# Two transformer stacks on one core: norms worked out by token tile behind the last pieces of the stage before, the token scale moved to the feed-forward's output, and new step orders

## The chip, the cores and the metric

The kernel runs on one core of a Trainium2 chip. A core has TensorE (PE, matrix products into eight PSUM banks), VectorE (DVE), ScalarE (ACT), GpSimd (POOL) and SyncE (SP, which issues transfers here); each follows its own list of instructions and they wait for each other by semaphores. The metric is the device time of one execution in microseconds, the median of the runs.

## The reference, cut to what matters

```python
def rms_norm(x, g):                      # x: 256 tokens x 1024, fp32
    return x * rsqrt(mean(x * x) + EPS) * g

for l in range(2):                       # first block
    x = x + 0.5 * swiglu(rms_norm(x, ffn1_norm[l]), w1, w3, w2)   # (silu(h@w1) * (h@w3)) @ w2, 2816 wide
    h = rms_norm(x, mix_norm[l]); z = h @ w_in[l]                 # 6752 columns
    ...                                  # neighbourhood attention, gated linear attention, latent attention
    x = x + mixed @ w_out[l]
    x = x + 0.5 * swiglu(rms_norm(x, ffn2_norm[l]), ...)
for l in range(2):                       # second block
    z = rms_norm(x, norm_g[l]) @ w_in_2[l]
    ...                                  # forgetting attention, convolution, compressed and sparse attention
    x = x + mixed @ w_out_2[l]
return rms_norm(x, final_g)
```

All of it is fp32. There are nine norms: three in each first layer, one in each second layer, one at the end.

## The kernel before, in words

All tokens stay in `x`, as two tiles of 128 tokens (t = 0, 1). A product in fp32 precision is made of three passes with operands split in a high and a low part (`passes`). Weights come in units of 1 MB through a ring of three slots (`Ring`): SP loads a unit into `raw` once the low part of the unit three before is made, ScalarE makes the high part (`hi`, line 391) once TensorE has used that slot, VectorE the low part (`lo`, line 402).

A norm (`Norm`) goes: ScalarE squares a tile and sums it; GpSimd makes 1/sqrt in two steps; VectorE scales the tile into `X`; TensorE transposes 8 pieces of each tile into four banks (`pe_transposes`); ScalarE writes the high part of each of the 8 blocks of 256 tokens, times the gain (`act_high`), and VectorE the low part (`dve_low`). The next stage waits for these block by block.

A feed-forward (`FFN`) goes over 11 pairs of units: w1 and w3 (`up_unit`, 48 matmuls of 256 columns each), then the w2 unit of the pair before (`down_unit`, 24 matmuls of 512). ScalarE makes Silu from PSUM, VectorE the product, both the high and low part of the hidden. The sums of x += 0.5 * result are four adds of 128x512 (`dve_add`).

The mixers run by orders written out by hand, one list for each engine (`PE1`, `ACT1`, `DVE1` for the first block's, `PE2`, `ACT2`, `DVE2` for the second's). A step is named with its number; a step that waits holds up all steps behind it in its list. `proj` and `tall` are projections by the normed tokens, `fv` one more (forgetting attention's v, 48 matmuls of 256 columns), `turn` are transposes of probabilities, `w_out` the output product, `x_add` its sum into x. In the second block `sg` is the turn of the sigmoid gates, `cmp_kv`, `cmp_score`, `cmp_turn` are the compressed branch, `taps` pieces of the convolution on VectorE (the other half is on GpSimd), `params` three small transposes of the layer's parameters, whose nine small transfers SP issues behind the load of `tall.0`.

Between two stages nothing is interleaved: the down or output products end, then adds, squares, scales, transposes and parts follow.

Of the kernel before, what the change touches and what calls it, by code (L numbers as in the profile page):

```python
# [25 lines left out]
K_ORDER = (0, 2, 4, 6, 1, 3, 5, 7)  # L26
# [90 lines left out]
def words(text):  # L117

    return [(w.split(".")[0], int((w + ".0").split(".")[1])) for w in text.split()]
# [7 lines left out]
def program(nc, A, out):  # L127
    ctx = ExitStack()
    with ctx:
# [4 lines left out]
        x = sb("x", [P, NT, D])  # L134
# [21 lines left out]
        ring = Ring(mem, s, 2 * RING_WIDTH1 + 2 * WIDTH2, 2 * RING_DMAS1 + 2 * DMAS2)  # L156
# [5 lines left out]
        with nc.Block() as block:  # L162
            @block.sync
            def _(sp):
                sp.dma_start(x[:, :, :], A["x"].rearrange("a (t p) d -> p (a t) d", p=P)).then_inc(s.x_in, 16)
                sp.dma_start(consts[:, :], A["consts"]).then_inc(s.consts_in, 16)
                for part in parts:
                    part.sync(sp)

            @block.tensor  # L170
            def _(pe):
                pe.wait_ge(s.consts_in, 16)
                for part in parts:
                    part.tensor(pe)

            @block.scalar
            def _(act):
# [3 lines left out]
                act.wait_ge(s.x_in, 16)  # L181
                for t in range(NT):
                    norm.act_squares(act, 0, t)
                act.wait_ge(s.consts_in, 16)
                act.activation(ident_r[:, :], C("ident"), ACT.Copy)
                act.activation(mask_r[:, :], C("causal"), ACT.Copy).then_inc(s.mask_ready, 1)
# [3 lines left out]
            @block.vector  # L190
            def _(dve):
                chain = Chain(dve, s.dve_chain)
                dve.memset(st[:, 255:256], -0.5)
                dve.memset(par[:, 8:768], 0.0).then_inc(s.cleared, 1)
                dve.wait_ge(s.x_in, 16)
                dve.wait_ge(s.consts_in, 16)
                for part in parts:
                    part.vector(dve, chain)
# [10 lines left out]
class Part:  # L209
# [19 lines left out]
    consts_in x_in cleared landed0 landed1 landed2 hi_ready lo_ready unit_used params0_in params_in  # L229
    rpb_copied rpb_in x_ready sumsq_ready rs_ready xn_ready xT_done hThi_ready hT_ready silu_ready gated  # L230
    hidhi_ready hid_ready acc0_done act_chain dve_chain pool_chain z_out na_squared na_summed na_rs
# [5 lines left out]
    mixed_ready mixhi_ready mix_ready wout0_done grs_ready gr_tanh krT_done kr_ready tok_out small_out  # L237
    sgT_done sg_ready tall_out tanh_out gate_ready paramT_done par_ready ff_in ff_log decay_ready bias_zero
# [8 lines left out]
    mlaT_done=6, state_done=6, half_done=6, pair_done=4, gla_done=1, oT_done=2, wout0_done=1, na_squared=4,  # L247
# [9 lines left out]
    cmp_done=1, kcmpT_done=1, cscore_done=1, cT_done=2, ln_done=3, wout0_done=1, tall_out=4, shifted=128,  # L257
    par_ready=1, small_out=1, blk_high=2, tanh_out=5, ff_log=1, a_exp=15, tok_out=2, gelu_tanh=2,
# [29 lines left out]
class Norm:  # L288
# [14 lines left out]
    def pool_rsqrt(self, pool, chain, n, t):  # L303
        m, s = self.m, self.s
        pool.wait_ge(s.sumsq_ready, 2 * n + t + 1)
        if n:
            pool.wait_ge(s.xn_ready, 2 * (n - 1) + t + 1)
        chain(pool.tensor_scalar(m["st"][:, 2 + t:3 + t], m["st"][:, t:t + 1], 1.0 / D, EPS, ALU.mult, ALU.add))  # L308
        pool.tensor_tensor(m["st"][:, 4 + t:5 + t], m["st"][:, 2 + t:3 + t], m["st"][:, 255:256],
                           ALU.pow).then_inc(s.rs_ready, 1)  # L310

    def dve_scale(self, dve, n, t):
        m, s = self.m, self.s
        dve.wait_ge(s.rs_ready, 2 * n + t + 1)
        dve.tensor_scalar(m["X"][:, 8192 + t * D:8192 + (t + 1) * D], m["x"][:, t, :],
                          m["st"][:, 4 + t:5 + t], None, ALU.mult).then_inc(s.xn_ready, 1)

    def pe_transposes(self, pe, n):
        m, s = self.m, self.s
        for t in range(NT):  # L320
            pe.wait_ge(s.xn_ready, 2 * n + t + 1)
            if n and t == 0:
                pe.wait_ge(s.x_ready, 2 * n)
            xn = m["X"][:, 8192 + t * D:8192 + (t + 1) * D].rearrange("p (q k) -> p k q", k=KK)
            for kk in range(KK):
                mm = pe.transpose(m["B"][4 + kk // 2][:, (kk % 2) * T + t * P:(kk % 2) * T + (t + 1) * P],  # L326
                                  xn[:, kk, :], m["C"]("ident"))
# [81 lines left out]
class FFN:  # L409
# [3 lines left out]

    def __init__(self, m, s, ring, f, u0, norm):
# [2278 lines left out]
```

## Time and profile before

| | us |
|---|---|
| median of 3 runs | 1752.14 (1747.67 to 1754.97) |
| profiled execution | 1750.93 |
| its span (first to last instruction) | 1749.1 |
| mean granted TensorE clock | 0.977 |
| TensorE busy | 1690.3 |
| VectorE busy | 1025.7 |
| ScalarE busy | 798.1 |
| GpSimd busy | 242.3 |

Busy times overlap each other. The clock is in shares of 2.4 GHz; the granted clock is either that or half of it, so a mean between tells how much of a stretch was at half. Waits are given with what released them.

### The profile page before, as it was taken

What the parts mean: (1) busy time and instruction counts of PE and PEld (TensorE: products, weight loads), DVE (VectorE), ACT (ScalarE), POOL (GpSimd) and SP (SyncE); (2) the same over time, 40 slices, a digit from 0 to 9 for tenths busy, and PEclk for the clock granted to TensorE, in tenths of its full rate; (3) what the DMA queues carried; (4) which work ended last, traced back from release to release, by engine and by line L of the source; (5) the groups of instructions that cost most, each with busy time, mean ns of one, the idle gap of its engine ahead of it and who ended that gap; (6) DMA issues with size and microseconds to landing.
All of it is one profiled execution on the core that took longest, in us unless ns stands there. A gap on an engine that the chain in (4) does not pass through costs nothing.

```text
span 1749.1 us, 26797 instructions
## 1 busy us (share of the span) xinstructions
PE 1690.3 (97%) x11146; PEld 1511.1 (86%) x11146; DVE 1025.7 (59%) x1162; ACT 798.1 (46%) x1049; POOL 242.3 (14%) x222
## 2 busy tenths in 40 slices
PE   7999999999999999999999999999999899989998
PEld 7999888889989998999978888989999888778885
DVE  4554557665654445454465764764445478746974
ACT  5433446643444434433455653454434454634553
POOL 0000230001000000000051010100000079003930
PEclk9999999999999999999999999999999889988998
DMA  7657455333555555656745242455555453245412
GB/s 231 213 176 231 149 173 163 121 118 101 176 161 193 177 183 159 195 178 201 221 138 187 91 145 73 169 169 193 175 185 175 130 171 103 89 136 157 150 50 85
DMA packets 207748, 275.02 MB, mean 157 GB/s; under 512 B 19014, under 2 KB 168232, under 8 KB 207144
## 3 DMA queue, kind: packets, MB, share of 16 engines
q1 hardware_dynamic: 206232, 272.67, 49.0%
q8 instruction: 66, 1.08, 0.3%
q10 hardware_dynamic: 1424, 1.05, 0.2%
q14 instruction: 26, 0.21, 0.0%
HBM read 271.61 MB, written 1.08 MB: 156 GB/s over the span
## 4 chain that ended last, share of the span: by engine, by line
PE 87%; DVE 7%; ACT 3%; ACTq 1%; issue 1%; DMA 0%; POOL 0%; SPq 0%; POOLq 0%; DVEq 0%
PE bank L467 29%; PE bank L480 13%; PE bank L854 9%; PE bank L843 7%; PE bank L1906 5%; PE bank L1039 4%; PE bank L2155 3%; DVE wlo L402 3%; ACT whi L391 2%; PE bank L1123 2%; PE bank L1884 1%; PE bank L2000 1%; PE bank L957 1%; PE bank L982 1%; PE bank L326 1%; PE bank L2058 1%
## 5 line engine op out<-in xcount | busy, mean ns | idle before, releaser
L402 DVE TENSOR_TENSOR wlo<-raw,whi 128x2048 fp32r<-128x2048 f32 (+1 forms) x258 | 583.2, 2264 | 452.3 <-ACT whi L391 451.5
L391 ACT ACTIVATE whi<-raw 128x2048 fp32r<-128x2048 f32 (+1 forms) x258 | 484.9, 1881 | 447.4 <-PE bank L467 129.0
L467 PE MATMUL bank<-hT_hi,whi 128*128 128x256 f32 x1408 | 400.2, 284 | 2.8 <-DVE hT_lo L342 2.8
L467 PE MATMUL bank<-hT_lo,whi 128*128 128x256 f32 x1408 | 399.7, 284 | 0.0
L467 PE MATMUL bank<-hT_hi,wlo 128*128 128x256 f32 x1408 | 399.5, 284 | 0.0
L467 PEld LDWEIGHTS bank<-hT_hi,whi 128*128 128x128 f32 x1408 | 271.4, 193 | 5.4 <-DVE wlo L402 2.6
L467 PEld LDWEIGHTS bank<-hT_lo,whi 128*128 128x128 f32 x1408 | 271.4, 193 | 1.4
L467 PEld LDWEIGHTS bank<-hT_hi,wlo 128*128 128x128 f32 x1408 | 271.4, 193 | 0.0
L480 PE MATMUL bank<-whi,Y 128*128 128x512 f32 x704 | 223.7, 390 | 0.0
L480 PEld LDWEIGHTS bank<-whi,Y 128*128 128x128 f32 x704 | 132.3, 188 | 26.7
L308 POOL TENSOR_SCALAR st<-st 128x1 f32<-128x1 f32 x18 | 4.4, 246 | 978.3 <-ACT X L299 971.2
L480 PE MATMUL bank<-wlo,Y 128*128 128x512 f32 x352 | 137.4, 390 | 0.0
L854 PE MATMUL bank<-hT_hi,whi 128*128 128x256 f32 x448 | 129.3, 289 | 0.4 <-ACT G L1179 0.4
L854 PE MATMUL bank<-hT_hi,wlo 128*128 128x256 f32 x448 | 126.7, 283 | 0.0
L854 PE MATMUL bank<-hT_lo,whi 128*128 128x256 f32 x448 | 126.7, 283 | 0.0
L516 ACT ACTIVATE X<-bank 128x512 f32<-128x512 f32 x44 | 26.3, 598 | 156.8 <-PE bank L467 156.8
L1906 PE MATMUL bank<-hT_hi,whi 128*128 128x256 f32 x288 | 87.0, 302 | 4.1 <-DVE wlo L402 4.1
L854 PEld LDWEIGHTS bank<-hT_hi,whi 128*128 128x128 f32 x448 | 85.7, 191 | 5.5 <-issue 3.8
L854 PEld LDWEIGHTS bank<-hT_lo,whi 128*128 128x128 f32 x448 | 85.8, 192 | 0.1
L854 PEld LDWEIGHTS bank<-hT_hi,wlo 128*128 128x128 f32 x448 | 85.8, 191 | 0.0
L1906 PE MATMUL bank<-hT_lo,whi 128*128 128x256 f32 x288 | 85.2, 296 | 0.0
L1906 PE MATMUL bank<-hT_hi,wlo 128*128 128x256 f32 x288 | 85.2, 296 | 0.0
(379 smaller groups left out, 2858.8 us busy)
## 6 DMA issues: line engine op xcount, KB each, us to landing
raw<-in_ffn_w SPq DMA_DIRECT2D x132, 1024.0 KB, 5.5
raw<-in_w_in SPq DMA_DIRECT2D x80, 1024.0 KB, 5.4
raw<-in_w_out SPq DMA_DIRECT2D x16, 1024.0 KB, 4.9
raw<-in_w_br_na SPq DMA_DIRECT2D x4, 1024.0 KB, 5.2
raw<-in_w_br_mla SPq DMA_DIRECT2D x4, 1024.0 KB, 5.7
raw<-in_w_br_gla SPq DMA_DIRECT2D x4, 1024.0 KB, 5.9
raw<-in_cmp_k_w SPq DMA_DIRECT2D x4, 1024.0 KB, 6.3
raw<-in_cmp_v_w SPq DMA_DIRECT2D x4, 1024.0 KB, 5.4
```

The lines of the kernel that those rows point to most:

```text
L326: mm = pe.transpose(m["B"][4 + kk // 2][:, (kk % 2) * T + t * P:(kk % 2) * T + (t + 1) * P], xn[:, kk, :], m["C"]("ident"))
L391: act.activation(m["whi"][:, slot, 0:w], m["raw"][:, slot, 0:w], ACT.Copy).then_inc(s.hi_ready, 1)
L402: dve.tensor_tensor(m["wlo"][:, slot, 0:w], m["raw"][:, slot, 0:w], m["whi"][:, slot, 0:w].bitcast(F32), ALU.subtract).then_inc(s.lo_ready, 1)
L467: mm = pe.matmul(B[bank][:, mt * T:(mt + 1) * T], a, b, start=(n == 0 and k == 0), stop=(n == KK - 1 and k == 2))
L480: mm = pe.matmul(B[4 + 2 * t + half][:, :], a, b, start=(start and mt == 0 and k == 0), stop=(last and mt == 1 and k == 2))
L516: act.activation(self.sil(par), B[par][:, :], ACT.Silu).then_inc(s.silu_ready, 1)
L843: mm = pe.matmul(B[bank + t][:, :], a, b, start=(h == 0 and k4 == 0 and k == 0), stop=(h == 1 and k4 == 3 and k == 2))
L854: mm = pe.matmul(B[bank][:, mt * T:(mt + 1) * T], a, b, start=(kk == 0 and k == 0), stop=(kk == KK - 1 and k == 2))
L1039: mm = pe.matmul(bank[:, m2 * T:(m2 + 1) * T], a, b, start=(kk == 0 and k == 0), stop=(kk == 3 and k == 2))
L1123: mm = pe.matmul(B[2 + 2 * t + half][:, :], a, b, start=(h == 0 and k2 == 0 and k == 0), stop=(h == 3 and k2 == 1 and k == 2))
L1906: mm = pe.matmul(B[bank][:, mt * T:(mt + 1) * T], a, b, start=(n == 0 and k == 0), stop=(n == KK - 1 and k == 2))
L2155: mm = pe.matmul(B[OUT_BANK[2 * t + half]][:, :], a, b, start=(first and k2 == 0 and k == 0), stop=(last and k2 == 1 and k == 2))
```

## The change

1. The norm works by token tile. Blocks of high and low parts have 128 tokens instead of 256, so there are 16 of each (step numbers i: tile i // 8, block K_ORDER[i % 8]); only the kernel's first norm keeps whole blocks. The order of the blocks is 0 2 1 3 4 6 5 7. Tile 1's transposes wait until all low parts of tile 0 are made. GpSimd's two steps become one: x has a further column of sqrt(D * EPS), squared and summed with the rest, and the square is scaled.
2. In front of a feed-forward the token scale is left out: x itself is transposed. The factor is applied inside: two matmuls (`token_scale`) spread the factors over the partitions, VectorE multiplies the w1 product by it (`scaled`) ahead of Silu, and the final add multiplies by it again in place of 0.5.
3. The last two down units are cut in pieces by tile and half (`dn.0` to `dn.7`), as are the output products (`wo.0` to `wo.15`), and each piece of the last unit has its own add. The first projection of the mixers (`pk`, and `fv` in the second block) goes tile by tile. Steps of the norm (`xt` transposes, `sq` squares, `scale`, `hh` high, `hl` low parts) stand in the lists between these.
4. At the start SP loads the identity (64 KB), the first weight unit, then x and the other constants.
5. All lists are written anew.

```diff
-K_ORDER = (0, 2, 4, 6, 1, 3, 5, 7)
+K_ORDER = (0, 2, 1, 3, 4, 6, 5, 7)
...
-                sp.dma_start(x[:, :, :], A["x"].rearrange("a (t p) d -> p (a t) d", p=P)).then_inc(s.x_in, 16)
-                sp.dma_start(consts[:, :], A["consts"]).then_inc(s.consts_in, 16)
+                sp.dma_start(C("ident"), A["consts"][:, 0:P]).then_inc(s.ident_in, 16)
...
+        act.activation(m["X"][:, 7167:8192], m["x"][:, t, :], ACT.Square, scale=float(D) ** -0.5 * (2 if half else 1),
                        accum_out=m["st"][:, t:t + 1]).then_inc(s.sumsq_ready, 1)
...
+    def pe_transposes(self, pe, n, t, banks, scaled=None):
+        if scaled is not None:
+            pe.wait_ge(s.xn_ready, 2 * scaled + t + 1)
+            src = m["X"][:, 8192 + t * D:8192 + (t + 1) * D]
+        else:
+            ...
+            src = m["x"][:, t, 0:D]
+        if n and t:
+            pe.wait_ge(s.hT_ready, 2 * KK * n + KK)
...
+    def act_high(self, act, n, i, banks, gain):
+        t, kk = i // KK, K_ORDER[i % KK]
+        act.wait_ge(s.xT_done, 8 * n + 4 * t + kk // 2 + 1)
+        if kk % 2:
+            act.wait_ge(s.hT_ready, 2 * KK * n + KK * t + K_ORDER.index(kk - 1) + 1)
+        act.activation(m["hT_hi"][:, kk, t * P:(t + 1) * P], self.xT(banks, kk, t), ACT.Copy,
...
+        def token_scale():
+            pe.wait_ge(s.rs_ready, 2 * self.norm + 2)
+            for t in range(NT):
+                mm = pe.matmul(B[self.scale_bank][:, t * P:(t + 1) * P], self.m["st"][:, 4 + t:5 + t].to_broadcast([P, P]),
+                               self.m["C"]("ident"), start=True, stop=True)
...
+            act.activation(self.sil(par), self.sil(par), ACT.Silu, scale=2.0).then_inc(s.silu_ready, 1)
...
+            dve.tensor_tensor(two(self.sil(par)), two(B[self.up[par]][:, :]), by, ALU.mult).then_inc(s.gate_scaled, 1)
...
+        dve.scalar_tensor_tensor(xs, self.m["B"][self.acc[t][half]][:, :], self.m["st"][:, 4 + t:5 + t], xs, ALU.mult,
+                                 ALU.add).then_inc(s.x_ready, 1)
...
+PE_JOIN = words("dn.0-2 dn.4-5 dn.3 xt.0 dn.6-7 xt.1")
+ACT_JOIN = words("hidh hi.0 hh.0-15 hi.1 sq.0-1")
+DVE_JOIN = words("hidl lo.0 add.0-1 hl.0-3 add.2 hl.4-7 add.3 hl.8-15 lo.1")
+PE_TURN = words("dn.0-2 dn.4-5 dn.3 dn.6-7")
+ACT_TURN = words("hidh hi.0 sq.0 hi.1")
+DVE_TURN = words("hidl lo.0 add.0-2 scale.0 add.3")
...
 PE1 = words("""
+    dn.0-2 dn.4-5 dn.3 dn.6-7 xt.0 pk.0-5 xt.1 pk.6-15 proj.1-3 small gq kr gla_up gk proj.4 lat proj.5 na_turn.0-1 gate.0
...
+    gate_b.11 branch.2 branch_b.2 branch.4 branch_b.4 branch.3 branch_b.3 branch.5 branch_b.5 wo.0-10 wo.12-13 wo.11 wo.14
+    xt2.0 wo.15 xt2.1
...
 ACT1 = words("""
+    hi.0 hidh sq.0 hi.1 hh.0-3 sq.1 hh.4-13 hi.2 hh.14-15 hi.3-5 proj.0 hi.6-7 proj.1-2 hi.8-9 proj.3 small hi.10 gq_out
...
+    hi.33 gate_out.11 gla_norm.3 hi.34 mix.0-1 hi.35-36 mix.2-4 hi.37 mix.5-7 hi.38-40 hh2.0-7 sq2.0 hh2.8-15 sq2.1
...
 DVE1 = words("""
+    hidl add.0-1 lo.0 scale.0 add.2-3 hl.0-3 lo.1 hl.4-5 scale.1 hl.6-13 lo.2 hl.14-15 lo.3-4 proj.0 lo.5-6 proj.1 lo.7-8
...
+    mix.5-7 lo.39 wadd.0-2 hl2.0-5 wadd.3 hl2.6-15 lo.40
...
 PE2 = words("""
-    tall.3 tall.4 params tall.0 sm tall.1 tall.2 w1.0 sg fv fox w1.1 tok.1 tok_b.1 w1.2 tok.0 w1.3 turn.0 tok_b.0 turn.1
-    turn.2 tall.5 heads_turn hid_turn value.0 cmp_kv score.3 score.4 score.5 cmp_score score.6 tall.6 turn.3 turn.4 score.7
-    turn.5 score.8 score.9 cmp_turn score.10 tall.7 score.11 tall.8 score.12 turn.6 ln.0 turn.7 turn.8 score.13 score.14
-    ln.1 turn.9 value.1 value.2 turn.10 ln.2 turn.11 turn.12 w_out.0 turn.13 turn.14 pw value.3 value.4 w_out.2 w_out.1
-    w_out.3
+    xt.0 params fv.0-6 xt.1 fv.7-15 tall.3-4 tall.0 sm tall.1-2 w1.0-1 fox sg tok.1 tok_b.1 w1.2 tok.0 w1.3 turn.0
+    tok_b.0 turn.1-2 tall.5 hid_turn cmp_kv heads_turn cmp_score tall.6 score.3-7 value.0 score.8 turn.3 score.9
+    cmp_turn turn.4-5 score.10 tall.7 score.11 tall.8 turn.6 score.12 turn.7 score.13 ln.0 turn.8 score.14 ln.1
+    value.1-2 ln.2 turn.9-10 wo.0 turn.11 wo.1-2 turn.12-13 wo.3 turn.14 value.3-4 pw wo.8-11 wo.4-6 wo.12-13 wo.7
+    wo.14-15
...
 ACT2 = words("""
-    hi.2 hi.3 hi.4 tall.0 hi.5 params sm hi.6 tall.1 blk.0 hi.7 tall.4 decay hi.8 tall.2 hi.9 hi.10 blk.1 fv hi.11 exp.0
...
-    turn.12 hi.21 out.1 ln_high hi.22 turn.13 turn.14 hi.23 conv_out hi.24 hi.25 out.2
+    hh.0 sq.1 hh.1-15 params hi.2-5 tall.4 tall.0 sm hi.6 hi.7 decay tall.1 blk.0 hi.8-9 blk.1 tall.2 hi.10-11 exp.0
...
+    ln_high turn.14 hi.23 conv_out hi.24 out.2
...
 DVE2 = words("""
...
-    lo.15 gelu_out.0 rotate gelu_out.1 taps.9 tall.5 lo.16 cmp_kv taps.10 peak.3 cmp_score peak.4 peak.5 lo.17 cmp_shift
...
+    hl.0-2 scale.1 hl.3-7 lo.1 hl.8-15 lo.2-5 sm lo.6 blk.0-1 lo.7 blk_low.0 decay lo.8 tall.4 fox_bias lo.9 taps.0-2
+    blk_low.1 peak.0 taps.3 sg lo.10 taps.4-5 peak.1 lo.11 taps.6-7 peak.2 taps.8 lo.12-13 prob.0 lo.14-15 gelu.0 taps.9
+    gelu_out.0 gelu.1 taps.10 rotate gelu_out.1 lo.16 cmp_kv cmp_score cmp_shift taps.11 tall.5 peak.3-4 cmp_prob peak.5-6
...
+    tall.7-8 ln.0 peak.13-14 ln.1 lo.20 prob.3-4 ln.2 ln_silu out.1 out_low.1 lo.21 ln_split conv_out lo.22 out.2 conv_low
+    lo.23-24 out_low.2
...
+        norm.act_squares(act, n0 + 1, 0)
+        ring.act_high(act, U0 + len(WIDTH2) + 1)
```

## Rows read from the trace of the kernel before

**Rows 1.** The page, part 1: busy time and share of each engine.

```profile
PE 1690.3 (97%) x11146; PEld 1511.1 (86%) x11146; DVE 1025.7 (59%) x1162; ACT 798.1 (46%) x1049; POOL 242.3 (14%) x222
```

**Rows 2.** Waits of TensorE: waiting line, releaser: us in total, times, longest.

```profile
PE bank L326 <- DVE X L315: 33.2, 12, 9.3
...
PE bank L2017 <- DVE KEEP L2366: 3.4, 2, 1.8
```

**Rows 3.** Windows over the seven joints: length, busy by engine, clock, DMA share, GB/s.

```profile
203.70:210.14 6.44, 3.27 (x17) 2.57 (x17) 3.47 (x7) 3.43 (x7) 1.64 (x4) 0.80 0.52 164
...
683.64:689.88 6.24, 2.32 (x17) 1.96 (x17) 3.46 (x7) 3.43 (x8) 1.64 (x4) 1.00 0.53 170
...
1356.74:1364.02 7.28, 3.08 (x16) 2.55 (x17) 4.30 (x7) 3.42 (x7) 3.48 (x6) 0.81 0.47 144
...
sum 46.51, PE 21.76 PEld 18.11 DVE 25.88 ACT 22.97 POOL 14.85; mean PE 3.11 PEld 2.59 DVE 3.70 ACT 3.28 POOL 2.12
```

**Rows 4.** Timeline of the first joint: start, length, instruction, count, idle before.

```profile
202.52 2.51 DVE L603 SCALAR_TENSOR_TENSOR x<-bank,x 128x512 f32<-128x512 f32 x4
...
203.84 1.06 ACT L299 ACTIVATE X<-x 128x1024 f32<-128x1024 f32 x1 [3.56 <-DVE x L603]
...
205.35 0.54 POOL L309 TENSOR_TENSOR st<-st 128x1 f32<-128x1 f32 x1
205.92 0.75 DVE L315 TENSOR_SCALAR X<-x,st 128x1024 f32<-128x1024 f32 x1 [0.89 <-POOL st L309]
...
206.73 3.43 PE L326 MATMUL bank<-consts,X 128*128 128x128 f32 x16 [3.03 <-DVE X L315]
...
209.00 3.14 ACT L336 ACTIVATE hT_hi<-bank,par 128x256 fp32r<-128x256 f32 x8 [2.73 <-PE bank L326]
209.51 3.25 DVE L342 SCALAR_TENSOR_TENSOR hT_lo<-bank,par,hT_hi 128x256 fp32r<-128x256 f32 x8 [1.37 <-ACT hT_hi L336]
```

**Rows 5.** Timeline of TensorE at the third joint, at the full clock.

```profile
686.67 1.16 PE L326 MATMUL bank<-consts,X 128*128 128x128 f32 x8 [3.03 <-DVE X L315]
688.14 1.16 PE L326 MATMUL bank<-consts,X 128*128 128x128 f32 x8 [0.31 <-DVE X L315]
689.88 0.35 PE L467 MATMUL bank<-hT_hi,whi 128*128 128x256 f32 x1 [0.59 <-DVE hT_lo L342]
```

**Rows 6.** The chain that ended last: start, length; one down unit of 24 matmuls.

```profile
56.96 5.47 PE bank L480 x24
```

**Rows 7.** The page, part 5: the low parts of the weights.

```profile
L402 DVE TENSOR_TENSOR wlo<-raw,whi 128x2048 fp32r<-128x2048 f32 (+1 forms) x258 | 583.2, 2264 | 452.3 <-ACT whi L391 451.5
```

**Rows 8.** Timeline of SP: first and last of nine parameter transfers, second block.

```profile
1345.44 0.56 SPq L1823 DMA_DIRECT2D par<-in_fox_b  x1
...
1349.37 0.42 SPq L1823 DMA_DIRECT2D par<-in_cmp_pe_v  x1
```

**Rows 9.** Timeline of the start.

```profile
10.40 1.91 ACT L391 ACTIVATE whi<-raw 128x2048 fp32r<-128x2048 f32 x1 [1.58 <-DMA raw<-in_ffn_w]
...
15.18 0.36 PE L467 MATMUL bank<-hT_hi,whi 128*128 128x256 f32 x1 [2.21 <-DVE hT_lo L342]
```

**Rows 10.** Groups by line and form: `ln.2`'s matmuls of broadcast factors; busy, mean ns.

```profile
L2123 PE MATMUL bank<-consts,st 128*128 128x128 f32 x8 | 1.2, 275 | 0.0
```

**Rows 11.** Timeline of TensorE, output product of the first second-block layer.

```profile
1544.87 0.47 PE L2155 MATMUL bank<-whi,Y 128*128 128x512 f32 x1 [3.40 <-DVE Y L2485]
```

**Rows 12.** Timeline of the end: last adds, last square.

```profile
1741.05 1.29 DVE L2592 TENSOR_TENSOR x<-x,bank 128x512 f32<-128x512 f32 x2 [1.43 <-PE bank L2155]
...
1742.71 1.06 ACT L299 ACTIVATE X<-x 128x1024 f32<-128x1024 f32 x1 [1.91 <-DVE x L2592]
```

**Rows 13.** Windows of 10 us, columns as in rows 3.

```profile
1460.00:1470.00 10.00, 10.00 (x86) 8.06 (x85) 9.56 (x30) 3.88 (x6) 9.61 (x9) 1.00 0.27 89
```

**Rows 14.** Timeline of VectorE: `prob.0` begins, `cmp_score` copies `kcT`.

```profile
1443.20 0.20 DVE L2461 RECIPROCAL st<-st 128x8 f32<-128x8 f32 x1
...
1470.88 0.38 DVE L2520 COPY KEEP<-bank 64x32 f32<-64x32 f32 x2
```

More of the change, by code:

```diff
@@ L117, in words @@
 def words(text):
-    return [(w.split(".")[0], int((w + ".0").split(".")[1])) for w in text.split()]
+    order = []
+    for w in text.split():
+        name, numbers = (w + ".0").split(".")[:2]
+        first, last = (numbers + "-" + numbers).split("-")[:2]
+        order += [(name, i) for i in range(int(first), int(last) + 1)]
+    return order
 def passes(left, right):
@@ L422, in landed, with sp @@
         return self.ring.loads_before(self.u0 + rel)
-    def sp(self, sp, l, w1, w3, w2, early=None, late=None):
+    def sp(self, sp, l, w1, w3, w2, early=None, late=None, start=None):
         r, u0 = self.ring, self.u0
@@ L811, in _ @@
                 ring.load(sp, u, (whole, w[:, :, 512 * (i % 2):512 * (i % 2) + 512]))
-            elif step == "w_out":
+            elif step == "wo" and i % 4 == 0:
                 w = layer("w_out").rearrange("a (k p) n -> p (a k) n", p=P)
-                for h in range(4):
-                    ring.load(sp, u + h, (whole, w[:, 2 * h:2 * h + 2, :]))
+                ring.load(sp, u, (whole, w[:, i // 2:i // 2 + 2, :]))
         ffn[1].sp(sp, l, A["ffn2_w1"], A["ffn2_w3"], A["ffn2_w2"], next_norm)
@@ L1129, in _, with w_out @@
-        steps = {"proj": proj, "small": lambda i: small(), "kr": lambda i: kr_turn(), "na_turn": na_turn, "score": score,
+        def w_out(n):
+            h, t, half = n // 4, n // 2 % 2, n % 2
+            slot = wait_unit(unit(("w_out", 0)) + h)
+            if n == 0:
+                pe.wait_ge(s.pT_ready, past.pT_ready + NA_HEADS + MLA_HEADS)
+                pe.wait_ge(s.y_ready, past.y_ready + 12)
+            pe.wait_ge(s.mix_ready, past.mix_ready + 2 * h + 2)
+            for k2 in range(2):
+                w = ring.w(slot, k2 * D + half * 512, 512)
+                for k, (a, b) in enumerate(passes(mx(2 * h + k2, t * P, P), w)):
+                    mm = pe.matmul(B[2 + 2 * t + half][:, :], a, b, start=(h == 0 and k2 == 0 and k == 0),
+                                   stop=(h == 3 and k2 == 1 and k == 2))
+            if n % 4 == 3:
+                mm.then_inc(s.unit_used, 1)
+            elif h == 3:
+                mm.then_inc(s.acc_done, 1)
@@ L1760 @@
 FIRST2, WIDTH2, DMAS2 = units2()
-W_OUT_ORDER = [h for step, h in PE2 if step == "w_out"]
+W_OUT_ORDER = [k // 4 for step, k in PE2 if step == "wo" and k % 4 == 0]
 def second_layer(nc, A, m, s, ring, norm, l):
@@ L1842, in _ @@
                 ring.load(sp, u, ((0, 512), layer("conv_pw").rearrange("a (k p) n -> p (a k) n", p=P)))
-            elif step == "w_out":
+            elif step == "wo" and i % 4 == 0:
                 w = layer("w_out").rearrange("a (k p) n -> p (a k) n", p=P)
-                ring.load(sp, u, (whole, w[:, 2 * i:2 * i + 2, :]))
+                ring.load(sp, u, (whole, w[:, i // 2:i // 2 + 2, :]))
             if step == "pw" and l + 1 < DEPTH:
```

586 lines of the change are left out of this document (311 added, 275 removed).

## Prediction

> **What bounds the kernel now.** I read the busy shares first. TensorE is busy for 97% of the span, VectorE for 59% [rows 1], so time can come out of TensorE's gaps or its low-clock stretches and hardly from anywhere else. Then who TensorE waits for: the largest entry is its transposes waiting for the scaled tokens, 33.2 us in 12 waits [rows 2]. Its longest, 9.3 us, is the kernel's start; the other 23.9 us lie at the seven places where one stage's output goes through a norm into the next. I cut one window per place, from the last matmul of a stage to the first projection matmul of the next: 46.51 us in all, in which TensorE shows 21.76 us of work, nearly all transposes [rows 3]. The timeline of the first place [rows 4] shows a serial chain: four adds, a square, two small GpSimd steps, a scale, 16 transposes, a high and a low part, 6.44 us for what is in itself 2.1 us of transposes (8 in 1.16 us at the full clock, [rows 5]). The granted clock falls in six of the seven, not in the third, which reads 1.00 with much the same idle time [rows 3].
>
> **The change, part by part.** One piece of a down or output projection is a quarter of 5.47 us, 1.37 us [rows 6]; a weight split costs VectorE 2.26 us [rows 7]; an add 0.63, a square 1.06 plus its read, the power 0.54, a scale 0.75 [rows 4]. From a tile's first transpose to the next stage's first matmul it was 1.74 us (688.14 to 689.88, [rows 5]).
>
> *First feed-forward into the mixer, twice.* Count from the end of the fifth piece (dn.5), which closes token tile 0; three pieces, 4.1 us, still follow. Tile 0's adds end at 0.65 and its square and power at 2.6, but VectorE has the split lo.0 in its order ahead of the scale: 2.95 to 3.7. That is still before 4.1, so xt.0 starts with no wait and the first pk matmul comes 1.75 us later. VectorE then does four low parts and lo.1 (2.3 us) before hl.4: pk.4 waits about 0.85. xt.1 follows scale.1 and hl.7, wait 0.15, and costs 1.05 itself. Together 3.8 us of TensorE time outside the 48 projection matmuls, against 6.44 and 6.69: **5.5 us saved**.
>
> *Mixer into the second feed-forward, twice.* Tile 0's transposes stand before wo.15 (1.05). After wo.15 xt2.1 must wait for all eight low parts of tile 0, with an add between them: 1.3. Then 1.75. That is 4.1 against 6.33 and 6.40: **4.5 us**.
>
> *Second feed-forward into the next first one, once.* No scale is left on the path. After dn.7: an add 0.7, then 1.75; xt.0 costs 1.05 earlier. But hi.1 now stands behind all 16 high parts, so lo.1 ends about 0.9 after the first up unit. 4.4 against 6.24: **1.8 us**.
>
> *Into each second layer, twice.* Same chain as the mixer's, but the piece of work between is short (fv: 0.36 us a step against a low part's 0.3 to 0.4), and sq.1 and scale.1 stand in the middle of tile 0's parts. I get 5.3 and 5.1 us beside the fv work, against 7.28 and 7.13: **4.0 us**. The params transposes are now behind xt.0. Their nine transfers are queued on SP after the load that waits for lo.0, and took 4.3 us to issue [rows 8], so they land about when TensorE asks; a further 1 to 2 us late would mostly hide in the low parts' own pace.
>
> *The price of half tiles.* The trace has high and low parts of 256 columns only, 0.39 and 0.41 us apart (3.14 and 3.25 for 8, [rows 4]). For 128 columns the bounds are half of that (0.2) and all of it. I take 0.3. At the upper bound each joint pays eight times 0.1 for its second tile, 0.8 us, 5 us over the kernel. The Trainium skill (ScalarE: Activation LUTs, What ACT_TABLE_LOAD costs) speaks against the split: an ACTIVATE has a fixed part of about 280 ns with a pointer operand beside 0.83 ns a column, and neighbours overlap by 93 ns. As an estimate from that page a half tile is 0.29 us, so 16 of them are 4.7 us of ScalarE where 8 whole ones took 3.14. It agrees with the row at 256 columns (0.40 by the page, 0.39 measured); no row shows 128.
>
> *Start.* Now unit 0 is ready late: its high part starts at 10.40, behind x and the constants, and the first matmul at 15.18 [rows 9]. With 64 KB of ident and then unit 0 ahead of x, x lands where unit 0 nearly did (about 9.5), by when the split of unit 0 is in work; no square, power or scale is in between. 16 transposes, then a high and low part: about 12.7. **2.5 us**, bounds 0 and 4. Unit 1 is not earlier than before, but is needed only after 5.8 us of unit 0.
>
> *Token scale.* Each of 4 feed-forwards gets two fp32 matmuls against ident; eight of that kind took 275 ns each [rows 10], about 0.4 a pair with its weight load: **-1.6 us**. The 44 extra multiplies on VectorE (0.69 each like the gating product) and the later Silu stay hidden: a pair of up units and a down unit take 17 us on TensorE, in which VectorE has under 9 of work. If that cover failed it would be 0.7 times 44, 30 us; I see no place for it, since bank and ring slack is over 2 us even in the first pair.
>
> *The output wait in the second layer.* TensorE waited 3.4 us for the last y [rows 11], because ScalarE had two weight splits ahead of it. Now one is ahead, but lo.24 is ahead on VectorE too; y comes about 5.1 us after wo.11, and 4.1 of output pieces cover it. **2.7 us**.
>
> *End.* One add of 0.63 instead of two stands in front of the last square (1741.05 and 1742.71, [rows 12]), and one GpSimd step less: **0.95 us**.
>
> *Orders inside the second layers.* The sg wait (3.4 us in two layers, [rows 2]) goes, since sg is early. But fv, 5.8 us of TensorE work, leaves the stretch in which VectorE is 96% busy [rows 13]. And the compressed branch now has little beside it. On VectorE it was 27.7 us from the first prob (1443.20) to the kcT copies (1470.88) [rows 14]; without the steps now elsewhere, about 23.3. TensorE's own steps there (turns, tok_b, tall.5, heads_turn) are 16.4, plus about 3 before them: some 4 us of waiting, where it was 2.15. I take **-2 us a layer, -4 in all**; bounds +2 and -15 a layer (cover wholly gone: 5.8, and 9 more at the compressed branch). In the mixers, whose inner waits are under 1.5 us each, I take nothing, bounds 2 either way.
>
> *Clock.* Of the low-clock stretches those behind the gaps cost some 8 us of slow work; I take **2 us** back, between 0 and 8.
>
> Sum: 2.5 + 5.5 + 4.5 + 1.8 + 4.0 - 1.6 + 2.7 + 0.95 - 4 + 2 = 18.35 us off the profiled execution's 1750.93, which is 1732.6. That execution lay 1.2 below the median of 1752.14, so I say **1734 us**.
>
> **The rivals.** *Joints close and the clock stays up.* For it: the third joint kept 1.00 through a wait of 3.03 us [rows 3, 5], and the new waits are all shorter. Against it: other gaps of the same length lost it. It gives the 8 us of clock instead of 2 and saves the second layers' 4: 1724. The Trainium skill (TensorE: Matmul & The Clock Gate, HAM oscillation — how this bites in real kernels) has the rule that short waits leave the clock up and only longer ones put the engine back to its half clock; by that the shortened joints would all run at 2.4 GHz. The trace agrees only in part: a wait of 3.03 us went with a fall at the first joint and with none at the third [rows 4, 5].
>
> *The joint doesn't do what it says.* The tokens are earlier, but VectorE, now with 16 parts, the adds and two or three weight splits in one order, becomes what TensorE waits for in the first projection. For it: splits of 2.3 us stand between low parts; my sum has 0.85 of this and it could be 2 to 3 in each. The seven then give 5 instead of 15.8, and the rest stays: 1745.
>
> *Slower: the second layers starve.* One mechanism: VectorE is the bound from the first prob to the compressed scores, and TensorE's cover there is gone. Price: 5.8 + 9 us a layer, and two low-clock stretches of 1.7 each: 36 us for two layers, against 4 in my sum. 1766. It decides from about 12 us a layer on. For it: VectorE at 9.56 of 10 us [rows 13]. Against it: before fv left, VectorE itself idled several us earlier in that stage waiting for TensorE, and those come forward.
>
> **How the numbers follow.** 0.67 for my sum, 0.13 for the first rival, 0.13 for the second, 0.07 for the slower one. Range 1722 to 1746: the low end is my sum with 8 us of clock and 4 more at the layers' inside, the high end the second rival. A measurement here can tell about 0.5%, 8.8 us: faster means below 1743.4. From the cases: faster 0.82, same 0.12, slower 0.06.
>
> **What would show it.** In the changed profile: per joint TensorE's time beside projection and output matmuls near 4 us, not 6.6; the first matmul near 12.7; no wait for a scaled tile over 1 us; a new wait of VectorE's low parts or wlo in pk; waits of 2 us or more at the compressed branch; feed-forward pairs still 16.98 us apart. Wrong if pairs are slower than that, or if the second layers' inner waits exceed 10 us.

## The result, and the profile after

The changed kernel took 1717.41 us (median of 4 runs, 1716.54 to 1718.62) where the kernel before took 1751.21 beside it: a ratio of 0.9821, interval 0.9802 to 0.9839. The forecast was 1734, and its range ended at 1722. So the sign was right and the gain, 34 us, about twice the 18 that were counted. The profiled executions tell the same: 1716.54 us with a span of 1714.7, against 1750.93 and 1749.1.

The busy shares of the changed kernel (name, us, share, instructions) answer to [rows 1]. TensorE has 26 us less to do although it runs 16 instructions more, and its idle time falls only from 58.8 us to 50.2 (span less busy time): closed gaps are the smaller part of it.

```profile
PE 1664.5 (97%) x11162; PEld 1475.2 (86%) x11162; DVE 1060.9 (62%) x1255; ACT 814.4 (47%) x1109; POOL 230.6 (13%) x204
```

TensorE's waits of the changed kernel (waiting line, releaser: us in total, times, longest), beside [rows 2]:

```profile
PE bank L333 <- DMA x<-in_x: 9.7, 1, 9.7
PE bank L2195 <- DVE KEEP L2624: 7.4, 2, 3.8
PE bank L2034 <- DVE wlo L435: 4.1, 2, 2.1
PE bank L333 <- DVE hT_lo L354: 3.7, 2, 1.8
...
PE bank L957 <- DVE hT_lo L354: 2.8, 6, 0.5
PE bank L333 <- DVE x L684: 1.5, 1, 1.5
```

The 33.2 us for the scaled tokens are gone, but for the load of x at the start (9.7). The new waits are those the forecast named: low parts of the tokens, and the compressed branch of the second layers (7.4 in two, where [rows 2] has 3.4 for another wait). The first joint shows it closely. This is TensorE's timeline there (start, length, instruction, count, idle before), to be held against [rows 4]:

```profile
200.38 1.16 PE L333 MATMUL bank<-consts,X 128*128 128x128 f32 x8
202.05 0.47 PE L957 MATMUL bank<-whi,hT_hi 128*128 128x512 f32 x1 [0.51 <-DVE hT_lo L354]
...
205.61 0.47 PE L957 MATMUL bank<-whi,hT_hi 128*128 128x512 f32 x1 [0.53 <-DVE hT_lo L354]
...
207.09 1.11 PE L333 MATMUL bank<-consts,X 128*128 128x128 f32 x8
```

From the first transpose to the end of the first projection's 48 matmuls it is 15.37 us (200.38 to 215.75, where the chain goes on with L975), of which the matmuls take 48 x 0.233: 4.2 us beside them, where the forecast had 3.8 and the kernel before 6.44. One half-tile low part takes 344 ns and two in a row 0.60, so 0.3 a piece, as was taken between the bounds of 0.2 and 0.4.

Then the surprise. This is a stretch of the chain inside a feed-forward (start, length, what), where of TensorE's work only the order of the k tiles and the banks differ, the order of the steps not:

```profile
60.35 11.20 PE bank L503 x96
71.56 5.60 PE bank L550 x24
77.15 2.92 PE bank L503 x25
```

Two up units, 96 matmuls of 256 columns, take 11.20 us. Before, the chain had this, and 5.47 for a down unit [rows 6]:

```profile
62.43 11.51 PE bank L467 x96
```

So 256-column products ran faster, 512-column ones slower, and a pair of up units with its down unit takes 16.80 us instead of 16.98, all through the feed-forwards.

### The profile page after: what moved, and what is told of

The parts are those of the page before. It is cut to its first block, busy times and chain, and to the rows that moved or that the text cites. A ratio compares the mean times of both kernels' runs of the same rounds, so it can differ in the third digit from the quotient of the medians.

```text
span 1714.7 us, 27114 instructions
## 1 busy us (share of the span) xinstructions
PE 1664.5 (97%) x11162; PEld 1475.2 (86%) x11162; DVE 1060.9 (62%) x1255; ACT 814.4 (47%) x1109; POOL 230.6 (13%) x204
## 4 chain that ended last, share of the span: by engine, by line
PE 83%; DVE 9%; ACT 4%; issue 2%; POOL 1%; ACTq 1%; DMA 0%; SPq 0%; POOLq 0%; DVEq 0%
PE bank L503 28%; PE bank L550 14%; PE bank L986 8%; PE bank L975 6%; PE bank L2034 4%; PE bank L1171 4%; DVE wlo L435 3%; PE bank L1253 2%; PE bank L2283 2%; ACT whi L424 2%; PE bank L2012 2%; PE bank L2129 1%; PE bank L1089 1%; DVE hT_lo L354 1%; PE bank L1074 1%
## 5 line engine op out<-in xcount | busy, mean ns | idle before, releaser
L503 PE MATMUL bank<-hT_hi,whi 128*128 128x256 f32 x1408 | 395.2, 281 | 1.5 <-DVE hT_lo L354 0.9
L503 PE MATMUL bank<-hT_lo,whi 128*128 128x256 f32 x1408 | 393.7, 280 | 0.0
L503 PE MATMUL bank<-hT_hi,wlo 128*128 128x256 f32 x1408 | 393.6, 280 | 0.0
L503 PEld LDWEIGHTS bank<-hT_hi,whi 128*128 128x128 f32 x1408 | 265.4, 188 | 4.9 <-issue 1.8
L503 PEld LDWEIGHTS bank<-hT_lo,whi 128*128 128x128 f32 x1408 | 265.3, 188 | 1.6
L503 PEld LDWEIGHTS bank<-hT_hi,wlo 128*128 128x128 f32 x1408 | 265.4, 188 | 0.0
L550 PE MATMUL bank<-whi,Y 128*128 128x512 f32 x704 | 228.0, 396 | 0.0
L308 POOL TENSOR_TENSOR st<-st 128x1 f32<-128x1 f32 x18 | 18.6, 1038 | 960.2 <-ACT X L301 960.2
L986 PE MATMUL bank<-hT_hi,whi 128*128 128x256 f32 x448 | 127.2, 284 | 0.1
L986 PE MATMUL bank<-hT_lo,whi 128*128 128x256 f32 x448 | 125.0, 279 | 0.0
L986 PE MATMUL bank<-hT_hi,wlo 128*128 128x256 f32 x448 | 125.0, 279 | 0.0
L572 ACT ACTIVATE X<-X 128x512 f32<-128x512 f32 x44 | 27.8, 633 | 172.0 <-DVE X L628 172.0
L986 PEld LDWEIGHTS bank<-hT_hi,whi 128*128 128x128 f32 x448 | 84.2, 188 | 3.7 <-issue 3.6
L2034 PE MATMUL bank<-hT_hi,whi 128*128 128x256 f32 x288 | 82.1, 285 | 4.1 <-DVE wlo L435 4.1
L986 PEld LDWEIGHTS bank<-hT_lo,whi 128*128 128x128 f32 x448 | 84.3, 188 | 0.1
L986 PEld LDWEIGHTS bank<-hT_hi,wlo 128*128 128x128 f32 x448 | 84.2, 188 | 0.0
L2034 PE MATMUL bank<-hT_lo,whi 128*128 128x256 f32 x288 | 81.1, 282 | 0.0
L2034 PE MATMUL bank<-hT_hi,wlo 128*128 128x256 f32 x288 | 81.0, 281 | 0.0
```

Source lines behind the costliest of these rows:

```text
L503: mm = pe.matmul(B[bank][:, mt * T:(mt + 1) * T], a, b, start=(n == 0 and k == 0), stop=(n == KK - 1 and k == 2))
L550: mm = pe.matmul(self.m["B"][self.acc[t][half]][:, :], a, b, start=(start and mt == 0 and k == 0), stop=(stop and mt == 1 and k == 2))
L572: act.activation(self.sil(par), self.sil(par), ACT.Silu, scale=2.0).then_inc(s.silu_ready, 1)
L986: mm = pe.matmul(B[bank][:, mt * T:(mt + 1) * T], a, b, start=(kk == 0 and k == 0), stop=(kk == KK - 1 and k == 2))
L2034: mm = pe.matmul(B[bank][:, mt * T:(mt + 1) * T], a, b, start=(n == 0 and k == 0), stop=(n == KK - 1 and k == 2))
```

## The experiments

Each run stands beside runs of the kernel before on the same chip; that one's medians lay between 1747.97 and 1750.04. "Up" below is the time of 96 up matmuls in the chain near 60 us, "down" that of 24 down matmuls.

**Where the tiles lie.** The change makes `x` one column wider in each of two token tiles: 8 bytes a partition. All tiles allocated behind it (hT_hi, hT_lo, X, G, Y and the rest) move by 8 bytes; raw, whi and wlo, ahead of it, stay. The other suspect was the new order of the k tiles.

```diff
 # e1, kernel before
         x = sb("x", [P, NT, D])
+        gap = sb("gap", [P, 2])
         hT_hi = sb("hT_hi", [P, KK, T], F32R)
 # e2, kernel before
-K_ORDER = (0, 2, 4, 6, 1, 3, 5, 7)
+K_ORDER = (0, 2, 1, 3, 4, 6, 5, 7)
```

> The kernel before with one edit: eight unused bytes a partition between x and hT_hi, so that every tile behind x stands 8 bytes later, as in the changed kernel. Its order, waits and counts are those of before. Theory A (the shift of the tiles sets the cadence of the matmuls): a unit of 48 up matmuls of 256 columns takes 5.60 instead of 5.755 us, the down unit of 24 matmuls of 512 columns 5.60 instead of 5.47, a pair 16.80 instead of 16.98; 44 pairs give -7.9 us and all three stages of the mixers a little more: 1740 to 1744 us. Theory B (the order of the k tiles, or the banks, or the day of the chip set it): 11.51 and 5.47 stay, 1750 to 1753 us.

> The kernel before with the k tiles of a matmul in the order 0 2 1 3 4 6 5 7 of the changed kernel, nothing else. Theory A (shift of the tiles): cadences stay at 11.51 us for two up units and 5.47 for a down unit, and the joints move by at most 0.3 us each: 1749 to 1753 us. Theory B (the order of the k tiles sets the cadence): 11.20 us for two up units and about 8 us less, 1741 to 1745 us.

Measured: e1 1741.02 us, ratio 0.9958 (0.9944 to 0.9972); e2 1747.82, 0.9991 (0.9974 to 1.0007). Eight unused bytes in the old kernel are worth 7 us by the ratio and 9 by the medians; the order of the k tiles nothing that can be told from zero. The chain of e1 has the changed kernel's pace to the hundredth:

```profile
61.74 11.20 PE bank L468 x96
72.94 5.60 PE bank L481 x24
```

The next two took the shift back in the changed kernel, by filling it up to 64 bytes.

```diff
 # e3, changed kernel
         x = sb("x", [P, NT, D + 1])
+        gap = sb("gap", [P, 14])
         hT_hi = sb("hT_hi", [P, KK, T], F32R)
 # e4, changed kernel
         hT_lo = sb("hT_lo", [P, KK, T], F32R)
+        gap = sb("gap", [P, 14])
         X = sb("X", [P, 10240])
```

> The changed kernel with 56 unused bytes a partition between x and hT_hi: x stays one column wider, and the tiles behind it stand a multiple of 64 bytes later than in the kernel before. Theory A: cadences go back to 11.51 us for two up units and 5.47 for a down unit, and the time rises by 8 to 12 us to 1725 to 1729. Theory B: 11.20 and 5.60 stay, 1716 to 1719 us.

> The changed kernel with the 56 unused bytes behind hT_lo instead: hT_hi and hT_lo keep their shift of 8 bytes, X, G, Y, KEEP and the constants stand again as in the kernel before. In an up unit hT is the moving side and whi the stationary one; in a down unit whi moves and Y is stationary. Theory A, with the shifted operand making the difference in either: up units stay at 11.20 us for two, the down unit goes back from 5.60 to 5.47 us, 44 down units give 5.7 us back: 1710 to 1713 us. Theory B: nothing changes, 1716 to 1719 us.

e3: 1739.99 us, 0.9952 (0.9935 to 0.9969), far slower than either theory expected; e4: 1720.94, 0.9851 (0.9826 to 0.9876), not faster. In e3 up is back at 11.51, but down stays at 5.60: it has the slow half of either kernel. The 512-column products of the projections, where hT is the stationary operand, are slow in it too: the 144 behind the mixers' first projection take 33.74 us in e3's chain and 32.66 in that of e7 below. So 64 bytes are not "where it was", and the suspect became the distance of the two operands. By the sizes of the tiles, those of the kernel before that TensorE reads here all begin at multiples of 8192 bytes; the addresses themselves were not read back. The next four put them there, or off it, in groups.

```diff
 # order of the allocations in the changed kernel; all but the marked at multiples of 8192 bytes
 # e5: raw whi wlo Y x | hT_hi hT_lo X G at +8
 # e6: raw hT_hi hT_lo X G Y gap(2) | whi wlo at +8 | x
 # e7: raw whi wlo hT_hi hT_lo X G Y x
 # e8: raw gap(2) | whi wlo hT_hi hT_lo X G Y at +8 | x
```

> The changed kernel with Y placed between wlo and x: whi, wlo and Y stand at multiples of 8192 bytes as in the kernel before, hT, X, G and all behind at 8 bytes past one. The run with 64 bytes (down unit 5.61, up 11.26) left open whether the 512-column matmuls look at Y's place or at something else. Theory A (each product's cadence is set by how its two operands stand to each other): two up units 11.20 us, the down unit back to 5.47, the mixer's projections (whi moving, hT stationary) stay at 5.60 for 24: 44 down units give 5.7 us back, 1711 to 1714 us. Theory B (the 512-column cadence was set by something that moved with all of it, the bias of the X or PSUM traffic for one): 5.60 stays, 1716 to 1719 us.

> The changed kernel with raw, hT, X, G and Y at multiples of 8192 bytes and whi and wlo 8 bytes past one, x behind them. Theory A, relative places: this is the same relation with the sign turned: two up units 11.20 us, down unit 5.60, 1716 to 1721 us. Theory C (only the place of the moving operand counts, and one off a 64-byte step is the faster): up units, where hT moves, go back to 11.51 us for two; 512-column matmuls, where whi moves, become no slower than 5.47 for 24: 1718 to 1726 us.

> The changed kernel with x placed behind Y, so that raw, whi, wlo, hT, X, G and Y all stand at multiples of 8192 bytes, as in the kernel before. Everything of the change is in it but the shift. Theory A: two up units 11.51 us, down unit 5.47, and the run comes 7 to 10 us behind the changed kernel: 1724 to 1729 us. Theory B (something else of the change made the matmuls faster): 1716 to 1719 us.

> The changed kernel with whi, wlo, hT, X, G and Y all 8 bytes past a multiple of 8192, raw alone at one and x behind Y. Theory A, relative places: operands stand to each other as before, so two up units 11.51 us and the down unit 5.47: 1724 to 1729 us. Theory C (absolute place of the moving operand): two up units 11.20 us, down unit at most 5.47: 1708 to 1714 us.

e5 1712.95 us, 0.9802 (0.9773 to 0.9831). e6 1729.25, 0.9887 (0.9858 to 0.9917). e7 1726.75, 0.9876 (0.9849 to 0.9902). e8 1726.26, 0.9876 (0.9850 to 0.9903). Theory A of relative places held three times; e8, with both operands moved by 8 bytes together, is as e7, which rules out the absolute place. e6 came out as neither theory said: minus 8 bytes is not the mirror of plus 8. The chain of e5, then of e7, then of e6:

```profile
60.00 11.20 PE bank L503 x96
71.20 5.46 PE bank L550 x24
```

```profile
60.86 11.51 PE bank L503 x96
72.37 5.47 PE bank L550 x24
```

```profile
60.99 11.36 PE bank L504 x96
72.36 5.60 PE bank L551 x24
```

Two more runs read four more distances, Y at 4 and 32 bytes, hT at 16 and 128.

```diff
 # e11: raw whi wlo gap(1) Y gap(3) hT_hi hT_lo X G x
 # e12: raw whi wlo gap(8) Y gap(24) hT_hi hT_lo X G x
```

> The changed kernel with whi and wlo at multiples of 8192 bytes, Y 4 bytes and hT 16 bytes past one, x behind them. It reads two more distances of operands at once. Theory A (distance modulo some small step sets it, 8 bytes being one sample): 256-column matmuls against hT at 16 bytes take 11.20 us for 96 or less, 512-column ones against Y at 4 bytes 5.60 for 24: 1716 to 1719 us. Rival (8 bytes is a special distance and 16 is as good as 0): 11.51 for 96, 1726 to 1730 us.

> The same with Y 32 and hT 128 bytes past a multiple of 8192. 64 bytes gave 11.54 us for 96 matmuls of 256 columns and 5.61 for 24 of 512 columns. Theory A: 128 bytes is like 64, 11.5 for 96, and 32 bytes for Y gives 5.60: 1730 to 1740 us. Rival (the cadence depends on a larger step, so 128 bytes may be another class): anything from 11.20 on, 1716 to 1722 us.

e11 1724.98 us, 0.9873 (0.9846 to 0.9900), between the ranges of its two theories; e12 1731.04, 0.9900 (0.9873 to 0.9926). For 256 columns the distances are graded, not two classes. All together, with the chain's time near 60 us (there the two runs at 64 bytes read 11.51 and 11.21, where the expectations above say 11.54 and 11.26):

| distance modulo 8192 bytes | up: hT against whi/wlo, 96 of 256 columns | down: Y against whi/wlo, 24 of 512 columns |
|---|---|---|
| 0 (before, e2, e7, e8) | 11.51 | 5.47 |
| +4 | | 5.59 to 5.60 (e11) |
| +8 (changed, e1; up also e4, e5) | 11.20 to 11.21 | 5.60 |
| -8 (e6) | 11.36 | 5.60 |
| +16 | 11.31 (e11) | |
| +32 | | 5.60 (e12) |
| +64 | 11.51 (e3) | 5.60 to 5.62 (e3, e4) |
| +128 | 11.39 (e12) | |

**The orders inside.** With e7 the cadence is out of the way: it is the change without the shift. Two runs undo one part of the orders each in it. e9 gives the mixers, from `small` to `branch_b.5`, the old orders on three engines; e10 gives the second layers the old ones from the GELU on.

```diff
 # e9, on e7 (TensorE's order; ScalarE's and VectorE's likewise)
-    gla_turn score.2 gate.1 turn.0 gate_b.1 score.3 turn.1 score.4 value.0-1 score.5 turn.2-3 gate.2
+    gla_turn score.2 turn.0 score.3 gate.1 gate_b.1 turn.1 score.4 value.0 turn.2 score.5 value.1 gate.2
...
 # e10, on e7
-    tok_b.0 turn.1-2 tall.5 hid_turn cmp_kv heads_turn cmp_score tall.6 score.3-7 value.0 score.8 turn.3 score.9
+    tok_b.0 turn.1 turn.2 tall.5 heads_turn hid_turn value.0 cmp_kv score.3 score.4 score.5 cmp_score score.6
...
```

> The run with x behind Y (same cadence of the matmuls as before, 1726.75 us, its profiled run 1726.8 of span) with the orders inside the two mixers, from the small projection to the last branch product, as the kernel before has them on TensorE, ScalarE and VectorE; joints, start and second layers stay new. Theory M (the new order inside the mixers is itself worth what the prediction had at nothing): from the fifth projection to the output projection TensorE takes 196.3 us again instead of 193.4 in each mixer, so 1732 to 1734 us. Rival (the 2.9 us a mixer come from the joint in front, which stages weights earlier): 193.4 stays and the run at 1726 to 1728 us.

> The run with x behind Y with the orders inside the two second layers as the kernel before has them from the GELU on (TensorE from the first transposed probabilities); the joints into them stay new. Theory S (as predicted: the new order costs about 2 us a layer through the later compressed branch, and takes most of the 3.4 us wait for y away): the waits for the compressed branch fall from 3.5 to 1.8 us a layer, the wait for y comes back, and the sum is 1723 to 1727 us. Rival (the new order is worth more than it costs): 1728 to 1733 us.

e9: 1734.30 us, 0.9924 (0.9897 to 0.9951). Theory M held, at the edge of its range (1732 to 1734): 7.5 us above e7 in the medians, 5.2 in the spans (1732.0 against 1726.8). The windows from the fifth projection to the output projection (length, TensorE busy, count, clock, DMA share, GB/s), first of e9, then of e7:

```profile
267.45:463.78 196.33, 195.59 (x1354) 1.00 0.39 125
```

```profile
266.95:460.35 193.40, 192.68 (x1354) 1.00 0.40 129
```

The same 1354 matmuls, at the same clock, with next to no idle time in either, and 2.9 us apart. The groups of that stretch show where most of it lies. Value products, in e9 and in e7 (busy us, mean ns), with the same length of one:

```profile
L1094 PE MATMUL bank<-X 128*64 128x256 f32 x32 | 6.2, 392 | 0.0
```

```profile
L1089 PE MATMUL bank<-X 128*64 128x256 f32 x32 | 5.1, 392 | 0.0
```

The state products (`upd`) fall from 6.3 to 5.3 in the same way and those of `gla_head` from 4.6 to 4.2; with the 1.1 here that is 2.5 of the 2.9 us. The timeline shows how. In e9 `value.0` and `value.1` stand apart:

```profile
310.82 1.08 PE L1094 MATMUL bank<-X 128*64 128x256 f32 x4
...
313.47 1.08 PE L1094 MATMUL bank<-X 128*64 128x256 f32 x4
```

In e7 they are neighbours (first line), and so are `upd.3` and `upd.4` (second line):

```profile
309.69 1.09 PE L1089 MATMUL bank<-X 128*64 128x256 f32 x8
...
376.27 1.13 PE L1196 MATMUL bank<-KEEP,G 64*128 64x256 f32 x8
```

Both value steps together take the time of one. In the code they write opposite halves of the partitions, and the two `upd` steps read opposite halves; one `upd` alone takes 1.13 in e9 (at 364.50). Being neighbours is not enough: `upd.0` and `upd.1`, on opposite halves too, stand together in e7 and take 1.89. This is read from the rows; no run moved one pair of steps alone.

e10: 1724.21 us, 0.9866 (0.9837 to 0.9895): 2.5 us under e7 in the medians, 5.0 in the spans. The intervals of e7 and e10 overlap, so that the new orders of the second layers cost something is likely, not shown, by these two. Waits of e10:

```profile
PE bank L2283 <- DVE Y L2608: 8.4, 3, 3.7
PE bank L2034 <- DVE wlo L435: 4.2, 3, 1.9
```

The wait for the compressed branch, 7.0 in e7, is gone altogether; the one for y is 8.4 instead of 1.0. One cost was traded for another of the same size. What is left of the 5.0 us is 2.7 of TensorE's busy time (1678.4 in e7, 1675.7 here) and 2.3 of idle time in smaller waits.

**The joints.** e13 changes TensorE's order alone, so that nothing lies between the two tiles' transposes.

```diff
 # e13, on e7
-PE_JOIN = words("dn.0-2 dn.4-5 dn.3 xt.0 dn.6-7 xt.1")
+PE_JOIN = words("dn.0-2 dn.4-5 dn.3 dn.6-7 xt.0-1")
-    dn.0-2 dn.4-5 dn.3 dn.6-7 xt.0 pk.0-5 xt.1 pk.6-15 proj.1-3 ...
+    dn.0-2 dn.4-5 dn.3 dn.6-7 xt.0-1 pk.0-15 proj.1-3 ...
-    ... wo.0-10 wo.12-13 wo.11 wo.14 xt2.0 wo.15 xt2.1
+    ... wo.0-10 wo.12-13 wo.11 wo.14-15 xt2.0-1
-    xt.0 params fv.0-6 xt.1 fv.7-15 ...
+    xt.0-1 params fv.0-15 ...
```

> The run with x behind Y (1726.75 us) with TensorE's order at the seven joints changed alone: both tiles are transposed behind the last product of the stage in front, and the next stage's first product comes only behind both, where the changed kernel has six of the last down matmuls' steps, or six of the first products of tile 0, between the two. VectorE's and ScalarE's orders and the norms tile by tile stay. Theory J (most of what the joints gave back is this overlap): a joint loses 1.0 to 2.5 us, seven of them 8 to 16, so 1734 to 1743 us. Rival (the joints gained by the shorter chain of norm and additions, not by the overlap on TensorE): under 0.5 us each, 1726 to 1730 us.

1752.65 us, 1.0029 (1.0012 to 1.0047). Theory J held in its sign and missed in its range, 1734 to 1743: the run lies 25.9 us above e7, 3.7 a joint, and is no better than the kernel before. In the spans it is 24.4 us, of which 17.0 are idle time of TensorE and 7.4 busy time, at a mean clock of 0.977 where e7 has 0.985. Waits of e13:

```profile
PE bank L333 <- DVE hT_lo L354: 25.7, 6, 5.5
...
PE bank L333 <- DVE x L684: 4.0, 1, 4.0
```

Tile 1's transposes go into the PSUM banks that tile 0's parts are read from, so they wait for all eight low parts of tile 0 (3.8 us of such waits in e7). Norms tile by tile without work between the tiles wait longer in this order, not shorter. The clock went along: windows over the first joint (columns as in e9's) of the changed kernel, then of e13:

```profile
197.00:217.00 20.00, 18.60 (x86) 1.00 0.43 135
```

```profile
200.00:220.00 20.00, 14.33 (x63) 0.83 0.42 136
```

**A version that beats both.** e14 has the places of e5, the old orders inside the second layers, and in VectorE's order there the low part of y, and that of the next weights, ahead of the gated convolution:

```diff
-ln_silu out.1 ln_split lo.21 conv_out lo.22 out_low.1 conv_low out.2 lo.23-24 out_low.2
+ln_silu out.1 ln_split out_low.1 lo.21 lo.22 conv_out conv_low out.2 lo.23 out_low.2 lo.24
```

> The changed kernel with three things: Y between wlo and x (1712.95 us, so that down units take 5.47 and up units 11.20), the orders inside the second layers of the kernel before (2.5 us less in the medians, 5.0 in the profiled runs), and in VectorE's order there the low half of the second y and the low half of the next weights put in front of the gated convolution, which takes away the two waits of 3.67 us for y that the old order left. Theory S: all three add up, 1701 to 1706 us. Rival (behind the wait for y stands the one for the weights' low half or the convolution, so only a third of it comes back): 1707 to 1711 us.

1702.55 us, 0.9741 (0.9720 to 0.9762), inside theory S's range. That is 14.9 us under the changed kernel's median and 10.4 under e5's, which has the same places. The old orders and the new place of the low parts were not run apart from each other on these places. The wait for the compressed branch and the one for y are both gone from its waits; the largest that are left, besides the load of x, are these:

```profile
PE bank L2034 <- DVE wlo L435: 5.0, 4, 2.0
PE bank L333 <- DVE hT_lo L354: 3.7, 2, 1.8
```

## Why the forecast was right in kind and wrong in size

Kernel before and e7 have the same pace of matmuls, so their chains can be laid side by side. The landmarks are the starts of the third pair of up units in each feed-forward, the fifth projection and the output projection in each mixer, and the last output matmul of each second layer. Us saved:

| step | forecast | before to e7 |
|---|---|---|
| start and first token scale | 2.5 - 0.4 | 1.6 (45.45 to 43.88) |
| feed-forward into mixer, two | 5.5 | 5.6 (2.9 and 2.7) |
| inside the mixers, two | 0 | 6.1 (2.9 and 3.2) |
| mixer into feed-forward, two, with scale | 4.5 - 0.8 | 3.0 (1.0 and 2.0) |
| feed-forward into feed-forward, with scale | 1.8 - 0.4 | 1.7 |
| first second layer: joint, inside, y | 2.0 - 2 + 2.7 | 3.7 |
| second second layer: joint, inside | 2.0 - 2 | -0.6 |
| end | 0.95 | 1.1 |
| clock | 2 | in the steps |
| sum | 18.35 | 22.3 |
| places of the tiles (e7 to changed) | none | 12.1 |

*The step that failed* is one of the last lines: "feed-forward pairs still 16.98 us apart". They came 16.80 apart, 44 of them, 7.9 us of the 12.1 that the places are worth in the profiled spans (9.3 in the medians, 1726.75 against 1717.41); the rest lies in the mixers and second layers. e7, the change without the shift, is at 1726.75, inside the forecast's range: it is the places that put the result below it. The one-column widening of `x` was read as a way to put the epsilon into the sum of squares and given no price. The forecast even named the pace as the thing that would make it wrong, but only upward.

*The second error* is "in the mixers ... I take nothing, bounds 2 either way". They gave 2.9 and 3.2 us, and e9 shows that it is the new order. The reasoning looked at TensorE's waits there, which were under 1.5 us, and not at the work itself, where neighbouring steps on opposite halves can overlap.

*A slip in the range.* From 1734, "8 us of clock" (6 more than counted) and "4 more at the layers' inside" give 1724, not the 1722 of the low end. The result lies below both.

*The joints* were near: 10.3 us measured for the five in front of mixers and feed-forwards where 10.6 were counted. The 10.3 contain what the clock gave back there, which the forecast booked apart, so the joints alone gave somewhat less. e13 shows that the work between the tiles is needed: without it the changed joints gain nothing. The rival "the joint doesn't do what it says" did not come: TensorE's waits for low parts in `pk`, which that rival put at 2 to 3 us a joint, are 2.8 us in six waits over both mixers.

*The start* gave 1.6 where 2.1 were counted. The first matmul comes at 13.46 (forecast 12.7, before 15.18, [rows 9]); from 10 to 20 us the clock is now 1.00, before 0.83.

*The second layers* were right in kind. The wait for the compressed branch is 3.7 a layer ("some 4 us"). The net price that e10 puts on the new orders, 2.5 to 5 us for both, is above the forecast's 4 less 2.7 for y. Nothing starved: the slower rival's stretch was covered.

*The clock* rose from 0.977 to 0.988 in the mean. The waits left in the changed kernel's joints are at most 1.84 us. That wait stands in both joints from a mixer into a feed-forward; here are windows of 10 us over them:

```profile
480.00:490.00 10.00, 7.83 (x49) 0.83 0.04 7
1140.00:1150.00 10.00, 7.83 (x59) 1.00 0.01 2
```

The same wait and the same busy time went with a fall in the first and with none in the second; the other joints show 1.00. In e13, with waits of 4 to 5.5 us, the clock fell again. The Trainium skill (TensorE: Matmul & The Clock Gate, HAM oscillation — how this bites in real kernels) says that it is long waits that cost the clock. The traces agree with the direction only: at one of the two joints 1.84 us of waiting, between the transposes of the two tiles, went with a fall.

## What to carry to other kernels

When an edit changes the size of a tile, list the tiles allocated behind it and count the change as a move of all of them; compare the pace of untouched back-to-back matmuls in both traces before explaining anything else. An order that works tile by tile pays through the work put between the tiles, so price that work first and the shorter chain second. An order without waits can still have time to give: look for steps that take less together than apart. When a new order removes one wait, look in the trace for the wait that takes its place, and try the order that has neither (e14).

## What the runs showed of the hardware

The pace of back-to-back fp32r matmuls depends on how far apart the moving and the stationary operand lie. At the full clock one of 256 columns takes 119.9 ns at distance 0 and 116.7 at 8 bytes; one of 512 columns 227.9 at distance 0 and 232.9 to 234.2 at the others tried with Y (4, 8, 32, 64 and -8 bytes). The range for a whole kernel is 27 us, 1.6%, between e3 (1739.99) and e5 (1712.95), which differ in nothing but unused bytes and the order of allocation. Which is better depends on the product: those of 256 columns were fastest off distance 0, those of 512 at it. The two kinds differ in their roles too (in the first the weights are stationary, in the second they move), and no run tells columns from roles. The Trainium skill (TensorE: Matmul & The Clock Gate, Step-by-step: what each phase is for) says that "Loading the next tile's weights doesn't steal SBUF read bandwidth from the running matmul"; taken alone, that gives no reason for the places to matter. The runs show that they do. Whether the weight load, the moving read or a third reader pays was not separated, and distances beyond 128 bytes were not tried.

GpSimd's power on one column takes 0.54 to 0.55 us in ten of its 18 places in the changed kernel and 1.33 to 1.88 in the other eight. All eight run beside VectorE's split of weights, none of the ten does. This is the first joint, GpSimd and then VectorE:

```profile
203.74 1.87 POOL L308 TENSOR_TENSOR st<-st 128x1 f32<-128x1 f32 x1 [4.20 <-ACT X L301]
...
202.93 2.28 DVE L435 TENSOR_TENSOR wlo<-raw,whi 128x2048 fp32r<-128x2048 f32 x1
```

The split ends at 205.21 and the power at 205.61; the other joints show the same 0.4 us between the two ends (487.13 + 1.88 against 486.32 + 2.28). So the power is done only once the split is. In the kernel before, none lies beside a split, and 17 of 18 take 0.54 to 0.56. By the orders it cost little here, as VectorE's scale stands behind the same split in its own list; what it cost was not run.
